# Decay masks of the state space groups fed from rows that a DMA spreads, and indexer pairs placed two units apart

## The chip, the core and the metric

The kernel runs on one core of one Trainium2 chip. A core has five engines that run their own instruction streams and meet only at semaphores: TensorE (PE in the tables; its weight loads are listed apart as PEld), VectorE (DVE), ScalarE (ACT), GpSimd (POOL) and SyncE (SP), which here only issues DMAs. The metric is the device time of one execution in microseconds (us), lower is better.

## The reference, cut to what matters

One encoder block: a feed-forward half step, a mixer, a second feed-forward half step, on 256 tokens of width 2048 in float32. The change lies in the mixer, in the state space branch and in the indexer of the attention branch:

```python
u = hn @ w_in
z, xbc, dt_raw, q, k, v, q_idx, k_idx, w_idx, gate_logits = _split_cols(u)
# state space branch: 32 heads in 8 groups of 4, state 128, head width 64
acum = jnp.cumsum(ac, axis=1)                      # ac = dt * a, one number for each token and head
seg = acum[:, :, None] - acum[:, None, :]
decay = jnp.exp(jnp.where(causal, seg, -jnp.inf))
cb = jnp.einsum('btgn,bsgn->btsg', cc, bc)
y_diag = jnp.einsum('btsg,btsgr,bsgrp->btgrp', cb, decay, xc)
# indexer: 16 heads of width 64, then the 64 best keys of each query
rel = jax.nn.relu(jnp.einsum('bthd,bsd->bths', qib, k_idx))
score = jnp.einsum('bths,bth->bts', rel, wb) * idx_scale
_, sel = lax.top_k(score, top_k)
```

The kernel does not scan over chunks of 64: for each group it builds the whole decay matrix from source token s to target token t in three blocks of 128x128 for each head (first half to first half, first half to second half, second half to second half) and multiplies once.

## The kernel before

**Weight units.** All large products stream their weights. A unit is 128 x 1024 float32 (512 KB). SP loads it into one of 4 `raw` buffers (L630) once VectorE has split the unit four earlier; ScalarE copies it to the high part `w_hi` (`cast`, L834) once TensorE has finished the unit four earlier; VectorE forms the low part `w_lo` (`sub`, L1298); TensorE then runs high*high, low*high and high*low, 12 matmuls of 512 columns for a unit with tokens on the partitions (`unit`, L2075 to L2077) or 24 of 256 columns for one with features on the partitions (`fm_unit`, L2376 to L2378). So VectorE can be at most some three units ahead of TensorE.

**The order of the side work.** Units are numbered; every engine walks the same numbers and has its side work written in at fixed ones. The mixer's input product takes 8 units for each block of 512 columns: b at 264, 274; c at 282, 290; xs at 298, 306, 314, 322; z at 330, 338, 346, 354; qi at 362, 370; k at 378; v at 386; q at 394, 402, 410, 418. Through unit 361 VectorE also adds up the modulation vectors (`ada_add`, L1318, weights loaded by L636) in about 10 of 16 units, with a `fold` at the end of each of them.

**A state space group g** starts at unit s = `ssd_start[g]` = 338, 346, 354, 362, 370, 378, 386, 394.
- TensorE at s: `ssd_products` makes the products of c and b (psum bank 4) and, with 8 small matmuls, the cumulated sums of the group's four heads (bank 5 and 6): the stationary operand is one column of `dta` broadcast over 128 columns, so that every partition gets the same row of cumulated sums. At s+5 `ssd_y` multiplies; at s+10 `turn_y` transposes, which first waits until the masks of group g+1 have left bank 4 (`seg_ready`).
- VectorE at s+2: `ssd_segments`, 12 operations of 128 columns that subtract the partition's own sum `acum` and cap at zero, from psum into `decay` (L1799), then three that take the products out of psum into `cb` (L1801 to L1803). At s+4 `ssd_mask`, at s+7 `ssd_gate`, at s+9 the norm, at s+12 `y_lo_out`.
- ScalarE at s+3: `decay_exp`, one exponential over all 1536 columns (L1160).

**The indexer** has 8 pairs of heads. Pair j: TensorE at `index_slot[j]` (4 matmuls into bank 5 and 6, after `rel_ready` j), ScalarE two units later (`index_relu`, after `score_step` 4j), VectorE three units later (`index_add`, four operations). The pairs stand at units 381 to 384 and 389 to 392; since they share banks 5 and 6 with the cumulated sums, `ssd_products` of groups 6 and 7 waits for `rel_ready` 4 and `head_ready`, and `index` for `seg_ready` 6 or 7. At 396 VectorE runs `admit`, and from 397 one of eight top-8 rounds a unit.

**Once, at unit 290**, `cumulate` makes the sums with tokens on the partitions (`acum`).

Of the kernel before, what the change touches and what calls it, by code (L numbers as in the profile page):

```python
# [113 lines left out]
def build(nc, x, c, positions, w_ada, b_ada, norm_ffn1, ffn1_w1, ffn1_w3, ffn1_w2, norm_mix, w_in,  # L114
# [94 lines left out]
    zs = place("zs", at_temp + 36 * KB, [GROUPS, HALF, T])  # L209
    yT_hi = place("yT_hi", at_temp + 20 * KB, [KT, T], F32R)  # L210
# [37 lines left out]
    gate_dram = nc.dram_tensor("gate_rows", (3, KT, P), F32).ap()  # L248
    h_dram = nc.dram_tensor("h_spill", (P, HALF, D), F32).ap()
# [80 lines left out]
    cb_ready = sem("cb_ready")  # L330
    seg_ready = sem("seg_ready")
# [60 lines left out]
    index_slot = ([start[at_block["k"]] + 3 + j for j in range(4)] + [start[at_block["v"]] + 3 + j for j in range(4)])  # L392
# [232 lines left out]
    def _(sp):  # L625
# [18 lines left out]
        for f in range(2):  # L644
# [32 lines left out]
            for n in range(MIX, M0):  # L677
                if n in FRONT_UNITS:
                    s = At(n).slot(RAW)
                    rows = slice((n - FRONT) * FRONT_KT * P, (n - FRONT + 1) * FRONT_KT * P)  # L680
                    dst = raw[:, s, 0:FRONT_KT * FRONT_COLS].rearrange("p (k n) -> p k n", k=FRONT_KT)
                    sp.wait_ge(split_ready, n + 1 - RAW)
                    sp.dma_start(dst[:, :, 0:SSD_H],
                                 w_in[0][rows, DT0:DT0 + SSD_H].rearrange("(k p) n -> p k n", p=P)).then_inc(front_in[n - FRONT], 16)
                    sp.dma_start(dst[:, :, SSD_H:],
                                 w_in[0][rows, KI0:G0].rearrange("(k p) n -> p k n", p=P)).then_inc(raw_in[s], 16)
                    continue
                load_unit(At(n), mix_source(n))
                if mixed_ada(n):
                    e, k = mixed_ada(n)  # L690
                    load_ada(At(e * KT + k), ada_source(e, k))
# [110 lines left out]
    def _(act):  # L802
# [277 lines left out]
        def xs_out(b):  # L1080
            i = WBLOCKS[b][1]
            act.wait_ge(xs_turned, i + 1)
            for half in range(HALF):
                ins = nc.scalar.activation(xs[:, 2 * i:2 * i + 2, half, :], by_group(4 + half), ACT.Copy)
            ins.then_inc(xs_ready, 1)
# [71 lines left out]

        def decay_exp(g):
            act.wait_ge(seg_ready, g + 1)
            nc.scalar.activation(decay[:], decay[:], ACT.Exp).then_inc(decay_ready, 1)  # L1160
# [49 lines left out]
        def mixer():  # L1210
            for n in range(MIX, M1):
                cast_units(n + 1)
                for b in range(NW):
# [18 lines left out]
                    if kind[b] == "k" and n == end[b] + 9:  # L1232
                        k_out()
# [6 lines left out]
                if n == FRONT_END + 11:  # L1240
                    kiT_out()
                for g in range(GROUPS):
                    s = ssd_start[g]
                    if n == s + 3:
                        decay_exp(g)
                    if n == s + 8:
                        y_square(g)
                    if n == s + 12:
                        y_hi_out(g)
# [42 lines left out]
    def _(dve):  # L1292
# [496 lines left out]
        def ssd_segments(g):  # L1789


            dve.wait_ge(cb_ready, g + 1)
# [4 lines left out]
            for j, bank, col in ((0, 5, 0), (1, 6, 2), (2, 6, 1)):  # L1797
                for k in range(4):
                    nc.vector.tensor_scalar(decay[:, j, k, :], psum[:, bank, k * P:(k + 1) * P],  # L1799
                                            acum[:, col, 4 * g + k:4 * g + k + 1], 0.0, ALU.add, ALU.min)  # L1800
# [172 lines left out]
        def mixer():  # L1973
            for n in range(MIX, M1):
# [14 lines left out]
                if n == FRONT_END + 2 * UPB + 2:  # L1989
                    cum_out()  # L1990
# [70 lines left out]
    def _(pe):  # L2061
# [339 lines left out]
        def turn_xs(b):  # L2401
            pe.wait_ge(conv_out, b + 1)
            i = WBLOCKS[b][1]
            if i:
                pe.wait_ge(xs_ready, i)
            for half in range(HALF):
                for k in range(4):
                    ins = turn(psum[:, 4 + half, k * P:(k + 1) * P], conv[:, k, half * P:(half + 1) * P])
            ins.then_inc(xs_turned, 1)

        def cumulate():

            pe.wait_ge(dta_ready, 1)
            pe.wait_ge(front_read, 1)
            for half in range(HALF):
                plain(psum[:, 4, half * SSD_H:(half + 1) * SSD_H], upper[:], dta[:, half, :])
            plain(psum[:, 4, 64:96], ones[:], dta[:, 0, :]).then_inc(cum_ready, 1)

        def ssd_products(g):
# [7 lines left out]
            if g == 6:  # L2427
                pe.wait_ge(rel_ready, 4)
            if g == 7:
                pe.wait_ge(head_ready, 1)  # L2430
            plain(psum[:, 4, 0:T], bT[:, g, 0:P], cT[:, g, :])
            plain(psum[:, 4, T:T + P], bT[:, g, P:T], cT[:, g, P:T])
            for half in range(HALF):
                for k in range(4):
                    ins = plain(psum[:, 5 + half, k * P:(k + 1) * P],
                                dta[:, half, 4 * g + k:4 * g + k + 1].broadcast_to((P, P)), upper[:])
            ins.then_inc(cb_ready, 1)
# [21 lines left out]
        def index(j):  # L2459
# [8 lines left out]
            pe.wait_ge(seg_ready, 6 if j < 4 else 7)  # L2468
# [79 lines left out]
        def mixer():  # L2548
            for n in range(MIX, M0):
                for b in range(NW):  # L2550
                    if kind[b] == "xs" and n == end[b] + 7:
                        turn_xs(b)
                    if kind[b] == "k" and n == end[b] + 7:
# [16 lines left out]
                if n == FRONT_END + 2 * UPB:  # L2570
# [107 lines left out]
```

## Time and profile before

| | |
|---|---|
| median of 3 runs | 2574.16 us (2573.16 to 2575.64) |
| the profiled execution | 2575.62 us, of which the span from first to last instruction 2573.9 us |
| PE busy | 2523.1 us, 98% |
| DVE busy | 1846.8 us, 72% |
| ACT busy | 1151.3 us, 45% |
| mean granted TensorE clock | 0.996 |

The span and what lies outside it (1.7 us) make up the profiled execution, which is 1.5 us above the median. A row's "busy" adds up the durations of instructions; those of matmuls overlap. Units 338 to 405 lie at about 1026 to 1275 us of the span.

### The profile page before, as it was taken

Reading aid. Unit: us, or ns where it says so; the run is one execution under the profiler, and the core shown is the slowest. Engines: PE = TensorE matmul, PEld = TensorE weight load, DVE = VectorE, ACT = ScalarE, POOL = GpSimd, SP = SyncE. Lnnn points to the kernel's source line nnn. Section 1 sums busy time; section 2 is a strip of 40 time slices with the busy share of each in tenths; the row PEclk is TensorE's granted clock in tenths of the full one; section 3 lists DMA queues with packets and bytes.
Section 4 is the critical chain, followed back from the end, with each engine's and each line's share of the span. In section 5 each row is a group of like instructions: output and inputs, shape, how many; then the busy total and the mean of one; then the engine's idle time right before and its main releaser. Section 6 shows DMA issues by size and latency. Waiting matters only on the chain.

```text
span 2573.9 us, 33768 instructions
## 1 busy us (share of the span) xinstructions
PE 2523.1 (98%) x12444; PEld 2127.6 (83%) x12444; DVE 1846.8 (72%) x2028; ACT 1151.3 (45%) x1365; POOL 114.2 (4%) x136
## 2 busy tenths in 40 slices
PE   7999999999998999999999999999999999999999
PEld 5878888888887999898788888887788888888887
DVE  5876678888976978967866677776779655555556
ACT  4444444344445555544455444443544444444443
POOL 4210000000002000000000000000300000000000
PEclk9999999999999999999999999999999999999999
DMA  9976679898977787654454788786499666666665
GB/s 372 384 249 194 188 264 344 293 342 293 343 238 227 246 293 262 212 164 124 143 145 138 229 277 263 256 288 231 133 314 336 192 191 189 191 190 189 192 190 173
DMA packets 279997, 610.15 MB, mean 237 GB/s; under 512 B 23426, under 2 KB 24004, under 8 KB 278980
## 3 DMA queue, kind: packets, MB, share of 16 engines
q1 hardware_dynamic: 268432, 567.22, 67.8%
q0 software_dynamic: 9744, 36.73, 3.8%
q10 hardware_dynamic: 1700, 4.58, 0.5%
q8 instruction: 77, 1.26, 0.2%
q14 instruction: 44, 0.36, 0.0%
HBM read 604.24 MB, written 4.22 MB: 236 GB/s over the span
## 4 chain that ended last, share of the span: by engine, by line
PE 90%; DVE 5%; DMA 2%; issue 1%; ACT 1%; POOL 0%; ACTq 0%; DVEq 0%; POOLq 0%
PE psum L2075 25%; PE psum L2077 25%; PE psum L2076 25%; PE psum L2376 3%; PE psum L2377 3%; PE psum L2378 3%; PE psum L2399 2%; PE psum L2063 2%; DMA raw<-in_ffn_w 1%; DVE w_lo L1298 1%; DVE ada_acc L1412 0%; DVE decay L1799 0%; ACT w_hi L834 0%; DVE score L1874 0%; DVE ada_acc L1318 0%
## 5 line engine op out<-in xcount | busy, mean ns | idle before, releaser
L1298 DVE TENSOR_TENSOR w_lo<-raw,w_hi 128x1024 fp32r<-128x1024 f32 x850 | 1034.8, 1222 | 524.3 <-ACT w_hi L834 523.3
L834 ACT ACTIVATE w_hi<-raw 128x1024 fp32r<-128x1024 f32 x850 | 897.6, 1060 | 1016.4 <-PE psum L2077 879.1
L2075 PE MATMUL psum<-w_hi,xT_hi 128*128 128x512 f32 x1984 | 785.6, 396 | 9.1 <-DVE w_lo L1298 4.0
L2077 PE MATMUL psum<-w_hi,xT_lo 128*128 128x512 f32 x1984 | 774.0, 390 | 0.0
L2076 PE MATMUL psum<-w_lo,xT_hi 128*128 128x512 f32 x1984 | 773.6, 390 | 0.0
L2075 PEld LDWEIGHTS psum<-w_hi,xT_hi 128*128 128x128 f32 x1984 | 373.4, 188 | 91.7 <-issue 15.3
L2077 PEld LDWEIGHTS psum<-w_hi,xT_lo 128*128 128x128 f32 x1984 | 373.1, 188 | 78.8
L2076 PEld LDWEIGHTS psum<-w_lo,xT_hi 128*128 128x128 f32 x1984 | 373.8, 188 | 75.8
L2075 PE MATMUL psum<-w_hi,aT_hi 128*128 128x512 f32 x704 | 274.8, 390 | 0.0
L2077 PE MATMUL psum<-w_hi,aT_lo 128*128 128x512 f32 x704 | 274.1, 389 | 0.0
L2076 PE MATMUL psum<-w_lo,aT_hi 128*128 128x512 f32 x704 | 274.0, 389 | 0.0
L1318 DVE SCALAR_TENSOR_TENSOR ada_acc<-ada_raw,cact,ada_acc 128x1024 f32<-128x1024 f32 x210 | 269.4, 1283 | 0.1
L2376 PE MATMUL psum<-xT_hi,w_hi 128*128 128x256 f32 x640 | 182.8, 286 | 6.3 <-DVE xT_lo L1457 5.7
L2377 PE MATMUL psum<-xT_lo,w_hi 128*128 128x256 f32 x640 | 181.1, 283 | 0.0
L2378 PE MATMUL psum<-xT_hi,w_lo 128*128 128x256 f32 x640 | 181.1, 283 | 0.0
L2077 PEld LDWEIGHTS psum<-w_hi,aT_lo 128*128 128x128 f32 x704 | 132.1, 188 | 27.6
L2075 PEld LDWEIGHTS psum<-w_hi,aT_hi 128*128 128x128 f32 x704 | 132.2, 188 | 27.4
L2076 PEld LDWEIGHTS psum<-w_lo,aT_hi 128*128 128x128 f32 x704 | 132.2, 188 | 27.2
L1517 DVE TENSOR_TENSOR y<-psum,y 128x1024 f32<-128x1024 f32 x93 | 113.6, 1221 | 31.5 <-PE psum L2077 31.5
L2376 PEld LDWEIGHTS psum<-xT_hi,w_hi 128*128 128x128 f32 x640 | 122.5, 191 | 7.5 <-DVE xT_lo L1457 6.5
L2377 PEld LDWEIGHTS psum<-xT_lo,w_hi 128*128 128x128 f32 x640 | 122.5, 191 | 0.0
L2378 PEld LDWEIGHTS psum<-xT_hi,w_lo 128*128 128x128 f32 x640 | 122.5, 191 | 0.0
(258 smaller groups left out, 1974.5 us busy)
## 6 DMA issues: line engine op xcount, KB each, us to landing
raw<-in_ffn_w SPq DMA_DIRECT2D x528, 512.0 KB, 4.5
ada_raw<-in_w_ada SPq DMA_DIRECT2D x224, 512.0 KB, 5.9
raw<-in_w_in SPq DMA_DIRECT2D x224, 512.0 KB, 3.9
ada_raw<-in_w_ada POOLq DMA_DIRECT2D x32, 512.0 KB, 7.5
ada_more<-in_w_ada POOLq DMA_DIRECT2D x32, 512.0 KB, 7.6
raw<-in_w_br_ssd SPq DMA_DIRECT2D x32, 512.0 KB, 5.2
raw<-in_w_br_att SPq DMA_DIRECT2D x32, 512.0 KB, 4.7
raw<-in_w_out SPq DMA_DIRECT2D x32, 512.0 KB, 5.4
```

Source lines behind the costliest of these rows:

```text
L834: nc.scalar.activation(w_hi[:, n.slot(SPLIT), 0:size], raw[:, n.slot(RAW), 0:size], ACT.Copy).then_inc(hi_ready, 1)
L1298: nc.vector.tensor_tensor(w_lo[:, n.slot(SPLIT), 0:size], raw[:, n.slot(RAW), 0:size], w_hi[:, n.slot(SPLIT), 0:size], ALU.subtract).then_ ...
L1318: nc.vector.scalar_tensor_tensor(out=acc[:], in0=src, scalar=cact[:, k:k + 1], in1=acc[:], op0=ALU.mult, op1=ALU.add).then_inc(ada_used, 1)
L1517: nc.vector.tensor_tensor(y[:, :, cols], psum[:, bank:bank + HALF, :], y[:, :, cols], ALU.add).then_inc(y_added, 1)
L2063: return nc.tensor.transpose(dst, src, ident[0:rows_, 0:rows_])
L2075: nc.tensor.matmul(o, hi[:, kt + k, toks], whi, start=a, stop=False)
L2076: nc.tensor.matmul(o, hi[:, kt + k, toks], wlo, start=False, stop=False)
L2077: ins = nc.tensor.matmul(o, lo[:, kt + k, toks], whi, start=False, stop=b)
L2376: nc.tensor.matmul(o, w_hi[:, s, cols], xT_hi[:, kt + k, :], start=a, stop=False, skip_group_check=True)
L2377: nc.tensor.matmul(o, w_hi[:, s, cols], xT_lo[:, kt + k, :], start=False, stop=False, skip_group_check=True)
L2378: ins = nc.tensor.matmul(o, w_lo[:, s, cols], xT_hi[:, kt + k, :], start=False, stop=b, skip_group_check=True)
L2399: return nc.tensor.matmul(o, a, b, start=first, stop=last)
```

## The change

The cumulated sums are made once, as 32 rows (one for each head) of 256 tokens: `cumulate` has two more products of `dta` (stationary) and `upper`, ScalarE copies them out (`cum_copy`, unit 292) and stores them to DRAM with a DMA of its own. For each group SP loads the group's four rows, 4 KB, into all 128 partitions (`cum_spread`, two buffers, 512 KB for each load), placed ahead of the load of unit s-2. The 8 matmuls for each group go. The first-to-second-half block, whose differences are never positive, goes to ScalarE as four exponentials with `acum` as the bias (`decay_off`); VectorE keeps 8 of its 12 operations, now from SBUF, and waits for TensorE's products only after them. The remaining exponential covers 1024 columns. The indexer pairs move to units 379, 381, ..., 393; the waits between them and the groups go, since banks 5 and 6 have no other user now, and the turn of k moves from unit 393 to 396.

```diff
-    index_slot = ([start[at_block["k"]] + 3 + j for j in range(4)] + [start[at_block["v"]] + 3 + j for j in range(4)])
+    index_slot = [start[at_block["k"]] + 1 + 2 * j for j in range(8)]
+    CUM_AT = FRONT_END + 2 * UPB
...
             for n in range(MIX, M0):
+                for g in range(GROUPS):
+                    if n == ssd_start[g] - 2:
+                        if g == 0:
+                            sp.wait_ge(cum_stored, 16)
+                        if g >= 2:
+                            sp.wait_ge(off_ready, g - 1)
+                            sp.wait_ge(seg_ready, g - 1)
+                        sp.dma_start(cum_spread[:, g % 2], cum_dram[4 * g:4 * g + 4, :].rearrange("(o r) n -> o r n", o=1)
+                                     .broadcast_to((P, 4, T))).then_inc(cum_in[g % 2], 16)
...
+        def cum_copy():
+
+            act.wait_ge(cum_ready, 1)
+            nc.scalar.activation(cum_rows[0:SSD_H, :], psum[0:SSD_H, 5, 0:T], ACT.Copy).then_inc(cum_copied, 1)
+            act.wait_ge(cum_copied, 1)
+            act.dma_start(cum_dram, cum_rows[0:SSD_H, :]).then_inc(cum_stored, 16)
+
+        def decay_off(g):
+
+            act.wait_ge(cum_in[g % 2], 16 * (g // 2 + 1))
+            act.wait_ge(acum_ready, 1)
+            if g:
+                act.wait_ge(y_raw, g)
+                act.wait_ge(masked_ready, g)
+            for k in range(4):
+                ins = nc.scalar.activation(decay[:, 1, k, :], cum_spread[:, g % 2, k, P:T], ACT.Exp,
+                                           bias=acum[:, 2, 4 * g + k:4 * g + k + 1])
+            ins.then_inc(off_ready, 1)
+
         def decay_exp(g):
+            decay_off(g)
             act.wait_ge(seg_ready, g + 1)
-            nc.scalar.activation(decay[:], decay[:], ACT.Exp).then_inc(decay_ready, 1)
+            nc.scalar.activation(decay[:, 0:3:2], decay[:, 0:3:2], ACT.Exp).then_inc(decay_ready, 1)
...
-            dve.wait_ge(cb_ready, g + 1)
+            dve.wait_ge(cum_in[g % 2], 16 * (g // 2 + 1))
             dve.wait_ge(acum_ready, 1)
             if g:
                 dve.wait_ge(y_raw, g)
                 dve.wait_ge(masked_ready, g)
-            for j, bank, col in ((0, 5, 0), (1, 6, 2), (2, 6, 1)):
+            for half in range(HALF):
                 for k in range(4):
-                    nc.vector.tensor_scalar(decay[:, j, k, :], psum[:, bank, k * P:(k + 1) * P],
-                                            acum[:, col, 4 * g + k:4 * g + k + 1], 0.0, ALU.add, ALU.min)
+                    nc.vector.tensor_scalar(decay[:, 2 * half, k, :], cum_spread[:, g % 2, k, half * P:(half + 1) * P],
+                                            acum[:, half, 4 * g + k:4 * g + k + 1], 0.0, ALU.add, ALU.min)
+            dve.wait_ge(cb_ready, g + 1)
...
             pe.wait_ge(dta_ready, 1)
+            pe.wait_ge(kiT_ready, 1)
             pe.wait_ge(front_read, 1)
             for half in range(HALF):
                 plain(psum[:, 4, half * SSD_H:(half + 1) * SSD_H], upper[:], dta[:, half, :])
+            for half in range(HALF):
+                plain(psum[0:SSD_H, 5, half * P:(half + 1) * P], dta[:, half, :], upper[:])
...
-            if g == 6:
-                pe.wait_ge(rel_ready, 4)
-            if g == 7:
-                pe.wait_ge(head_ready, 1)
             plain(psum[:, 4, 0:T], bT[:, g, 0:P], cT[:, g, :])
-            plain(psum[:, 4, T:T + P], bT[:, g, P:T], cT[:, g, P:T])
-            for half in range(HALF):
-                for k in range(4):
-                    ins = plain(psum[:, 5 + half, k * P:(k + 1) * P],
-                                dta[:, half, 4 * g + k:4 * g + k + 1].broadcast_to((P, P)), upper[:])
-            ins.then_inc(cb_ready, 1)
+            plain(psum[:, 4, T:T + P], bT[:, g, P:T], cT[:, g, P:T]).then_inc(cb_ready, 1)
...
-            pe.wait_ge(seg_ready, 6 if j < 4 else 7)
...
-                    if kind[b] == "k" and n == end[b] + 7:
+                    if kind[b] == "k" and n == end[b] + 10:
                         turn_k(b)
```

TensorE's queue around units 389 to 394 before (`kiT,qiT` is a pair of the indexer, `ident,qn` the turn of k, `cT,bT` the products of group 7, `upper,dta` its cumulated sums; between the marks stand the unit's own matmuls):

```order
L2399 MATMUL psum<-xdt,decay 128x64 x12
L2399 MATMUL psum<-kiT,qiT 128x256 x4
L2075 MATMUL psum<-w_hi,xT_hi 128x512
...
L2063 MATMUL psum<-ident,qn 128x128 x8
L2075 MATMUL psum<-w_hi,xT_hi 128x512
...
L2399 MATMUL psum<-cT,bT 128x256
L2399 MATMUL psum<-cT,bT 128x128
L2399 MATMUL psum<-upper,dta 128x128 x8
L2075 MATMUL psum<-w_hi,xT_hi 128x512
```

The same place in the changed kernel:

```order
L2440 MATMUL psum<-xdt,decay 128x64 x12
L2440 MATMUL psum<-kiT,qiT 128x256 x4
L2116 MATMUL psum<-w_hi,xT_hi 128x512
...
L2440 MATMUL psum<-cT,bT 128x256
L2440 MATMUL psum<-cT,bT 128x128
L2116 MATMUL psum<-w_hi,xT_hi 128x512
...
L2104 MATMUL psum<-ident,qn 128x128 x8
L2104 MATMUL psum<-ident,yg_137 128x128 x4
```

The eight `upper,dta` are gone, and the turn of k stands behind the products of group 7 now.

VectorE's queue before, from unit 394 to the start of 397 (`score` is the indexer's sum, `cb` and `decay` belong to group 7, `banned` and `dist` to `admit`):

```order
L1874 SCALAR_TENSOR_TENSOR score<-rel,wi,score 128x256 x4
L1298 TENSOR_TENSOR w_lo<-raw,w_hi 128x1024
L1838 TENSOR_SCALAR yg_135<-yg,y_rstd 128x256 x2
L1874 SCALAR_TENSOR_TENSOR score<-rel,wi,score 128x256 x4
L1298 TENSOR_TENSOR w_lo<-raw,w_hi 128x1024
L1799 TENSOR_SCALAR decay<-psum,acum 128x128 x12
L1801 TENSOR_TENSOR cb<-psum,upper 128x128
L1802 COPY cb<-psum 128x128
L1803 TENSOR_TENSOR cb<-psum,upper 128x128
L1893 TENSOR_SCALAR banned<-key_chunk,query_chunk 128x256 x2
```

And in the changed kernel:

```order
L1915 SCALAR_TENSOR_TENSOR score<-rel,wi,score 128x256 x4
L1338 TENSOR_TENSOR w_lo<-raw,w_hi 128x1024
L1879 TENSOR_SCALAR yg_137<-yg,y_rstd 128x256 x2
L1338 TENSOR_TENSOR w_lo<-raw,w_hi 128x1024
L1839 TENSOR_SCALAR decay<-cum_spread,acum 128x128 x8
L1842 TENSOR_TENSOR cb<-psum,upper 128x128
L1843 COPY cb<-psum 128x128
L1844 TENSOR_TENSOR cb<-psum,upper 128x128
L1915 SCALAR_TENSOR_TENSOR score<-rel,wi,score 128x256 x4
L1934 TENSOR_SCALAR banned<-key_chunk,query_chunk 128x256 x2
```

The last pair's sum now stands behind the masks of group 7, right ahead of `admit`, and four of the twelve mask operations are gone.

SP's queue at the first of the eight new loads:

```order
L638 DMA raw<-in_w_in 128x2x512
L693 DMA cum_spread<-cum_rows 128x1024
L638 DMA raw<-in_w_in 128x2x512
L644 DMA ada_raw<-in_w_ada 128x1024
L638 DMA raw<-in_w_in 128x2x512
```

The new load stands between two weight loads of the same queue.

## Rows read from the trace of the kernel before

**Rows 1.** The page: busy time (share) and instructions; the chain by engine.
```profile
PE 2523.1 (98%) x12444; PEld 2127.6 (83%) x12444; DVE 1846.8 (72%) x2028; ACT 1151.3 (45%) x1365; POOL 114.2 (4%) x136
...
PE 90%; DVE 5%; DMA 2%; issue 1%; ACT 1%; POOL 0%; ACTq 0%; DVEq 0%; POOLq 0%
```

**Rows 2.** Windows: us, then PE, PEld, DVE, ACT, POOL busy (count), clock, DMA share, GB/s.
```profile
860.00:1000.00 140.00, 140.00 (x1171) 140.00 (x1170) 120.95 (x173) 74.63 (x96) 0.00 (x0) 1.00 0.79 265
...
1020.00:1060.00 40.00, 40.00 (x212) 34.31 (x211) 34.54 (x59) 21.02 (x27) 1.78 (x2) 1.00 0.81 276
...
1026.10:1300.00 273.90, 268.34 (x1571) 231.62 (x1570) 217.44 (x407) 132.30 (x184) 16.21 (x22) 1.00 0.54 164
...
1053.46:1081.00 27.54, 27.54 (x147) 23.53 (x146) 23.91 (x39) 14.96 (x20) 1.76 (x2) 1.00 0.72 233
```

**Rows 3.** Timeline around group 0: start, us, engine, line, names [idle before, releaser].
```profile
1026.10 0.85 PEld L2399 LDWEIGHTS psum<-cT,bT 128*128 128x128 f32 x4
...
1026.87 1.87 PEld L2399 LDWEIGHTS psum<-upper,dta 128*128 128x128 f32 x16
...
1028.66 0.19 PEld L2075 LDWEIGHTS psum<-w_hi,xT_hi 128*128 128x128 f32 x1
...
1028.97 3.19 DVE L1799 TENSOR_SCALAR decay<-psum,acum 128x128 f32<-128x128 f32 x12 [1.88 <-PE psum L2399]
...
1032.79 1.49 ACT L1160 ACTIVATE decay<-decay 128x1536 f32<-128x1536 f32 x1 [2.93 <-DVE cb L1803]
```

**Rows 4.** TensorE's timeline, units 355 to 404: the waits that another engine ended.
```profile
1089.39 0.30 PE L2063 MATMUL psum<-ident,yg 128*128 128x128 f32 x1 [0.54 <-DVE cb L1803]
...
1192.33 0.49 PE L2399 MATMUL psum<-kiT,qiT 64*128 64x256 f32 x2 [0.26 <-ACT rel L1155]
...
1207.67 0.30 PE L2063 MATMUL psum<-ident,yg 128*128 128x128 f32 x1 [0.61 <-DVE cb L1803]
...
1227.80 0.49 PE L2399 MATMUL psum<-kiT,qiT 64*128 64x256 f32 x2 [2.10 <-ACT rel L1155]
...
1232.86 0.30 PE L2063 MATMUL psum<-ident,qn 128*128 128x128 f32 x1 [0.94 <-ACT rel L1155]
...
1263.53 0.39 PE L2076 MATMUL psum<-w_lo,xT_hi 128*128 128x512 f32 x1
1263.75 0.39 PE L2077 MATMUL psum<-w_hi,xT_lo 128*128 128x512 f32 x1
1264.87 0.47 PE L2075 MATMUL psum<-w_hi,xT_hi 128*128 128x512 f32 x1 [0.73 <-DVE w_lo L1298]
...
1274.16 0.50 PE L2075 MATMUL psum<-w_hi,xT_hi 128*128 128x512 f32 x1 [0.39 <-DVE w_lo L1298]
```

**Rows 5.** VectorE's timeline at units 395 and 396; last row: two scalings in SBUF.
```profile
1235.36 1.67 DVE L1874 SCALAR_TENSOR_TENSOR score<-rel,wi,score 128x256 f32<-128x256 f32 x4
...
1239.16 3.20 DVE L1799 TENSOR_SCALAR decay<-psum,acum 128x128 f32<-128x128 f32 x12 [0.99 <-PE psum L2399]
...
1077.95 0.60 DVE L1838 TENSOR_SCALAR yg<-yg,y_rstd 128x256 f32<-128x256 f32 x2
```

**Rows 6.** DMA issues, KB, us to landing; last row: all DMAs of gate_rows.
```profile
raw<-in_w_in SPq DMA_DIRECT2D x64, 512.0 KB, 3.7
ada_raw<-in_w_ada SPq DMA_DIRECT2D x10, 512.0 KB, 6.0
...
DMA to landing us min/median/max: 3.3/6.3/8.3
```

**Rows 7.** Groups by form: xcount, busy us, mean ns, idle before.
```profile
L1165 ACT ACTIVATE yg<-yg 128x256 f32<-128x256 f32 x14 | 5.7, 412 | 15.4 <-DVE yg L1833 15.4
...
L834 ACT ACTIVATE w_hi<-raw 128x1024 fp32r<-128x1024 f32 x65 | 68.4, 1057 | 36.0 <-PE psum L2077 21.4 <-PE psum L2378 14.4
```

**Rows 8.** Windows behind the mixer, at the half-clock stretch.
```profile
1790.00:1795.00 5.00, 2.60 (x10) 2.11 (x11) 1.94 (x6) 2.17 (x4) 0.61 (x1) 0.50 0.40 118
1795.00:1800.00 5.00, 5.00 (x13) 3.85 (x13) 0.74 (x1) 0.00 (x0) 0.28 (x1) 0.50 0.95 397
```

More of the change, by code:

```diff
@@ L209, in build @@
     zs = place("zs", at_temp + 36 * KB, [GROUPS, HALF, T])
+    cum_rows = place("cum_rows", at_temp + 22 * KB, [T])
+    cum_spread = place("cum_spread", at_temp + 76 * KB, [2, 4, T])
     yT_hi = place("yT_hi", at_temp + 20 * KB, [KT, T], F32R)
@@ L248, in build @@
     gate_dram = nc.dram_tensor("gate_rows", (3, KT, P), F32).ap()
+    cum_dram = nc.dram_tensor("cum_rows", (SSD_H, T), F32).ap()
     h_dram = nc.dram_tensor("h_spill", (P, HALF, D), F32).ap()
@@ L330, in build @@
     cb_ready = sem("cb_ready")
+    cum_copied = sem("cum_copied")
+    cum_stored = sem("cum_stored")
+    cum_in = [sem("cum_in0"), sem("cum_in1")]
+    off_ready = sem("off_ready")
     seg_ready = sem("seg_ready")
@@ L1082, in xs_out @@
             act.wait_ge(xs_turned, i + 1)
+            act.wait_ge(cum_stored, 16)
             for half in range(HALF):
@@ L1231, in mixer @@
                             head_squares(1 + WBLOCKS[b][1], b)
-                    if kind[b] == "k" and n == end[b] + 9:
+                    if kind[b] == "k" and n == end[b] + 12:
                         k_out()
@@ L1241, in mixer @@
                     kiT_out()
+                if n == CUM_AT + 2:
+                    cum_copy()
                 for g in range(GROUPS):
@@ L1988, in mixer @@
                     dt_rest(n - FRONT_END - 7)
-                if n == FRONT_END + 2 * UPB + 2:
+                if n == CUM_AT + 2:
                     cum_out()
@@ L2403, in turn_xs @@
             i = WBLOCKS[b][1]
-            if i:
-                pe.wait_ge(xs_ready, i)
+            pe.wait_ge(xs_ready, i) if i else pe.wait_ge(cum_copied, 1)
             for half in range(HALF):
@@ L2569, in mixer @@
                     ins.then_inc(ki_turned, 1)
-                if n == FRONT_END + 2 * UPB:
+                if n == CUM_AT:
                     cumulate()
```

## The prediction

> **What bounds the kernel now.** I read the page first: TensorE is busy for 98% of the span and carries 90% of the chain that ended last [rows 1]. Then the windows over the changed stretch, units 338 to 405: of 273.9 us TensorE is busy for 268.3, VectorE for 217.4, ScalarE for 132.3, at full granted clock [rows 2]. Then TensorE's timeline, for what it waits for there: seven waits, 5.57 us in all [rows 4]. Three end with ScalarE's `rel` (0.26, 2.10, 0.94), the chain of an indexer pair in which TensorE, ScalarE and VectorE take turns at one unit's distance; two with VectorE's `cb` (0.54, 0.61), where `turn_y` waits for the masks of the next group; two with `w_lo` (0.73, 0.39), where VectorE is truly the bound, in the top-8 rounds. So in this stretch a matmul removed is time removed, as long as VectorE keeps up, and five of the seven waits belong to chains that the change touches.
>
> A rule speaks against reading it so. The Trainium skill, Perfetto Trace Analysis, section Identifying the Most-Contended Engine, says that matmul busy time is a poor measure of headroom and that LDWEIGHTS busy should be used; that is 231.6 of 273.9 us here, so by it TensorE would have 42 us free and a removal might bring nothing. It is rival D below; the trace doesn't side with it, since the waits add up to 5.57 us only.
>
> **The change part by part.**
>
> *The eight small matmuls of each group go.* Around group 0 their weight loads begin at 1026.87 and the next unit's first one at 1028.66 [rows 3]: 1.79 us for 8 matmuls (16 records, two for each). Nothing lies over them: TensorE goes straight on. 8 groups x 1.79 = **14.3 us off the path**.
>
> By the Trainium skill, TensorE: Matmul & The Clock Gate, section Back-to-back issue gap, matmuls of 128 columns follow each other at about 81 ns; 8 x 16 of them would be an estimated 10.4 us. The trace's own distance, 112 ns, is what I use.
>
> *Added on TensorE:* two more products in `cumulate`, 128 columns each, four records at the same 0.112 us: 0.45 us, taken as **0.5 us added**. Its new wait for `kiT_ready` names a step that ScalarE does five units earlier: nothing.
>
> *The waits in which TensorE stood for the pairs and masks* [rows 4]. The three with `rel`: a unit is 12 matmuls, 0.22 us apart (starts 1263.53 and 1263.75), so 2.7 us. A pair now has two units (5.5 us) until the next instead of one, and what must fit between is one ScalarE relu of 1024 columns (as a cast of as many, 1.06 us [rows 7]), the four sums of 1.67 us [rows 5], and the unit's own cast and split, 1.06 and 1.2. That is 5.0 in a row: too long for 2.7, short enough for 5.5. The turn of k, which waits for the last pair, moves back three units. The two with `cb`: VectorE's mask work for a group was 3.19 us after a wait for TensorE's products (1.88 us at group 0, 0.99 at group 7) [rows 3, 5]. Now it need not wait and does 8 of 12 operations. So I let all five go: 4.45 us, and with each the refill of the pipeline. That shows at the wait of 0.73 us: starts 1263.75 and 1264.87 are 1.12 apart where 1263.53 and 1263.75 are 0.22 apart, so the stop costs 0.9, 0.17 more than the wait. 5 x 0.16 = 0.8. Together **5.25 us**; the bounds are 0 (other turns come last, rival B) and 5.25.
>
> *VectorE's share, at the two waits with `w_lo`.* An operation from psum costs 3.19 / 12 = 0.27 us. From SBUF the trace has the same operation with twice the columns at 0.60 for two, 0.30 each [rows 5]. So one of 128 columns costs at most 0.27 and at least half of it, 0.13; I take 0.2, nearer the wider SBUF row less its columns. 8 x 0.2 = 1.6 against 3.2: 1.6 us less a group (bounds 1.1 and 2.1). In the stretch to 1264 VectorE gains the 0.99 wait and 1.6, but the last pair's sum (1.67) now stands inside it, behind the masks of group 7, while TensorE arrives 1.79 earlier. Counted from the same split that is 0.9 gained against 1.79 needed: the wait would grow by 0.9. But that split began at 1236.95 only because the pair's sum at 1235.36 had just ended [rows 5]; with the sum moved, it can begin up to 1.6 us sooner. Net 0.7 better. The two waits with refill are 1.44 us; I take half, **0.7 us**, with 0 and 1.44 as bounds, and down to -1 if the split does not come sooner.
>
> *ScalarE.* The one exponential of 1490 ns becomes four of 128 columns and one of 1024. 256 columns take 412 ns and 1024 take 1057 [rows 7], so 128 take about 0.3: 1.2 + 1.06, 0.8 us more a group. The four lie in the 2.93 us in which ScalarE waited for the masks [rows 3]; behind them stand the casts of the next units, which get 0.4 us earlier. Cost nothing; without that cover 0.8 x 8 on an engine that is half idle. Once, at unit 292, `cum_copy` and its DMA issue, 0.4 us by the row of 256 columns [rows 7] and an issue that has no row, say up to 1 us: ScalarE is busy for 75 of 140 us there and TensorE for all of it [rows 2]. Nothing.
>
> *SP and the DMAs.* Eight more loads of 512 KB, 4.2 MB. Same size: 3.7 us to landing for weights, 6.0 for the modulation's, and 8.3 for the slowest of the gate rows, the only transfers here that spread small DRAM rows over the partitions [rows 6]. The new load stands behind the load of unit s-3, which waits for the split of s-7, and it is read at s+2: nine units, 24 us. SP's own new waits name masks two groups old; the weight loads queued behind them are not held. The DMA engines are busy for 0.81 of the time in the fullest window [rows 2]; a load for every 8 units adds under 0.1. Nothing; what it costs if the spread is slow is rival E.
>
> *Sum:* 14.3 - 0.5 + 5.25 + 0.7 = 19.75 us. From the profiled execution, 2573.9 span + 1.7 around it = 2575.6, that gives 2555.9; the shown median is 1.5 lower, so **2554.4 us**.
>
> **The rivals.**
>
> A, the forecast, 2554.4; own range 2552.5 to 2557. Chance 0.62.
>
> B, the matmuls' time comes but the waits don't: VectorE is the next engine. For it: in the window of groups 1 and 2 it is busy for 23.9 of 27.5 us [rows 2], and TensorE's share shrinks to 25.7; against it: its own shrinks to some 22.3. Without the 5.95 us of waits: 2574.2 - 13.8 = 2560.4, up to 2562. Chance 0.18.
>
> C, the clock behind the mixer. From 1790 to 1800 the granted clock is 0.50, the lower of its two levels (1.2 GHz); TensorE is idle for 2.4 of the first 5 us and works for 7.6 of the 10 [rows 8], so the stretch costs 3.8 us. Shifted by 20 us it may fall elsewhere or not at all: 2550.6, or 2558.2 if it gets longer. Chance 0.12.
>
> D, the change takes work from an engine that has room: 2574. For it only PEld's 85%, against it the sum of waits. Chance 0.04.
>
> E, slower: all partitions read the same 4 KB. Unit n's weights are asked for when n-4 is split, at best three units (8.2 us) ahead, and take 3.7, so 4.5 us are spare. If a spread holds the queue for x us, TensorE stops for x - 4.5 each time. Gain and loss balance at x = 4.5 + 19.75 / 8 = 7.0; at 8.3, the slowest of rows 6, it is 8 x 3.8 = 30 us: 2585. Against it: that row holds twice the bytes in 512 B pieces. Chance 0.04.
>
> **How the numbers follow.** The likeliest case gives 2554.4. The range reaches over C's gain and B's loss: 2550.5 to 2562.5, which leaves out D, E and the ends of A to C, under 2 in 10. About 0.2% (5 us) is what a measurement of this kernel can tell from no change; A, B and C all lie beyond it: faster 0.92, same 0.04 (D), slower 0.04 (E).
>
> **What would show it.** In the profile after, TensorE's timeline should have the next unit's first weight load some 0.7 us behind the start of each group's products, not 2.5; no wait for `rel`, and none for `cb`; VectorE's masks in 1.6 us or so with no wait for TensorE ahead; the spread loads landing within 8 us and no cast that waits for a weight DMA in this stretch. A wait for `w_lo` longer than 1 us between 1230 and 1270 would speak for B, a half-clock stretch of another length behind the mixer for C, casts released by a weight DMA at the groups for E. The forecast is wrong if VectorE's operations from SBUF cost as much as from psum and the stops in the top-8 rounds grow.

## The result, and the profile after

The changed kernel takes **2555.15 us** (median of 4 runs, 2553.68 to 2555.81); the kernel before, run beside it, 2573.93 (4 runs, 2573.16 to 2575.64). The ratio is 0.9925 (95% interval 0.9913 to 0.9937): faster by 0.75%, 18.8 us. The forecast was 2554.4.

The page of the changed kernel, busy time and chain by engine, against [rows 1]:

```profile
PE 2507.5 (98%) x12320; PEld 2113.5 (83%) x12320; DVE 1834.7 (72%) x1996; ACT 1158.0 (45%) x1398; POOL 114.0 (4%) x136
...
PE 91%; DVE 5%; DMA 2%; issue 1%; ACT 1%; POOL 0%; ACTq 0%; DVEq 0%; POOLq 0%
```

TensorE and VectorE have less to do (15.6 and 12.1 us), ScalarE more (6.7), and TensorE still carries the chain.

**Where the time went.** The records of single products mark points of the two traces. Products of `c` and `b` and logits (`kT,qT`), before: name, count, ns, first and last start.

```profile
L2399 PE MATMUL psum<-kT,qT x64: 377/379/382, 1289.0 to 1404.4; 128*128 128x256 f32 x64
...
L2399 PE MATMUL psum<-cT,bT x32: 271/326/381, 1026.3 to 1237.1; 128*128 128x256 f32 x16, 128*128 128x128 f32 x16
```

The same in the changed kernel, with the products of `cumulate`:

```profile
L2440 PE MATMUL psum<-kT,qT x64: 377/379/382, 1268.7 to 1384.1; 128*128 128x256 f32 x64
...
L2440 PE MATMUL psum<-cT,bT x32: 271/326/381, 1025.8 to 1218.9; 128*128 128x256 f32 x16, 128*128 128x128 f32 x16
...
L2440 PE MATMUL psum<-upper,dta x4: 272/273/297, 884.5 to 884.8; 128*32 128x128 f32 x4
```

From the products of group 0 to the first logits, which I call **the stretch** below, it is 1289.0 - 1026.3 = 262.7 us before and 1268.7 - 1025.8 = 242.9 after: 19.8 us. The forecast has one term ahead of the stretch, the added products in `cumulate` at unit 290. To take it in, count from the first turned block of activations (`ident,act_tok`, at 190.1 us before and 188.9 after), which lies ahead of all that was changed: to the first logits it is 1098.9 us before and 1079.8 after, **19.1 us** for the whole change, against 19.75 in the forecast. (The two profiled executions, 2575.62 and 2555.07, lie 20.55 apart, of which 1.2 us arose ahead of 190 us, where the two kernels do the same; the medians lie 18.8 apart. The last section says where totals move while these distances don't.)

Windows of the changed kernel, as in [rows 2] and [rows 8]: us, PE, PEld, DVE, ACT, POOL busy (count), clock, DMA share, GB/s.

```profile
1020.00:1060.00 40.00, 40.00 (x198) 33.72 (x197) 35.18 (x56) 26.08 (x38) 1.77 (x2) 1.00 0.89 310
1026.10:1281.00 254.90, 253.82 (x1447) 218.19 (x1446) 205.41 (x375) 139.89 (x219) 15.98 (x22) 1.00 0.59 190
...
1770.00:1775.00 5.00, 2.72 (x13) 2.01 (x14) 2.51 (x4) 2.17 (x4) 0.61 (x1) 0.58 0.64 204
1775.00:1780.00 5.00, 5.00 (x18) 4.00 (x17) 0.00 (x0) 1.06 (x1) 0.56 (x1) 0.74 0.85 345
```

In these windows over the groups and the indexer TensorE is idle for 1.1 us, where it was for 5.6. The fullest window's DMA share rose from 0.81 to 0.89. The stretch at the lower clock behind the mixer is still there, but the second window is already back at 0.74 where it was 0.50: it lasts 6.8 us instead of 10.2.

Timeline around group 0 of the changed kernel, against [rows 3]:

```profile
1025.61 0.84 PEld L2440 LDWEIGHTS psum<-cT,bT 128*128 128x128 f32 x4
1025.83 0.81 PE L2440 MATMUL psum<-cT,bT 128*128 128x256 f32 x4
1026.37 0.19 PEld L2116 LDWEIGHTS psum<-w_hi,xT_hi 128*128 128x128 f32 x1
...
1026.50 1.65 DVE L1839 TENSOR_SCALAR decay<-cum_spread,acum 128x128 f32<-128x128 f32 x8
...
1029.37 1.28 ACT L1191 ACTIVATE decay<-cum_spread,acum 128x128 f32<-128x128 f32 x4
1030.56 1.05 ACT L1198 ACTIVATE decay<-decay 128x1024 f32<-128x1024 f32 x1
```

The next unit's first weight load stands 0.76 us behind the products' first one, where it stood 2.56 behind (1026.10 and 1028.66 in [rows 3]): 1.80 less. VectorE's masks take 1.65 us instead of 3.19 and have no wait ahead of them; ScalarE's four exponentials take 1.28 and the wide one 1.05, instead of 1.49 in one.

All of TensorE's waits for other engines in the stretch, against the seven of [rows 4]; each line ends with total us, times, longest.

```profile
PE psum L2104 <- DVE cb L1844: 0.8, 1, 0.8
PE psum L2116 <- DVE w_lo L1338: 0.3, 1, 0.3
```

**The sum closes.** The eight groups' matmuls are worth 14.3 us (8 x 1.79). The waits, each with the 0.16 of refill that the prediction takes from the wait of 0.73, were 5.57 + 7 x 0.16 = 6.7 before and are 0.81 + 0.27 + 2 x 0.16 = 1.4 after, so 5.3. Together that is 19.6 of the 19.8.

**The one wait that stayed** is the turn of group 1's `y` at unit 356, and it grew from 0.54 to 0.81. VectorE's timeline there, changed kernel; the last row is TensorE's:

```profile
1075.28 1.23 DVE L1338 TENSOR_TENSOR w_lo<-raw,w_hi 128x1024 fp32r<-128x1024 f32 x1 [0.96 <-ACT w_hi L851]
1076.42 1.28 DVE L1358 SCALAR_TENSOR_TENSOR ada_acc<-ada_raw,cact,ada_acc 128x1024 f32<-128x1024 f32 x1
1077.73 0.45 DVE L1376 STREAM_TRANSPOSE fold_tmp<-ada_acc 128x256 f32<-128x256 f32 x1
...
1081.36 1.65 DVE L1839 TENSOR_SCALAR decay<-cum_spread,acum 128x128 f32<-128x128 f32 x8
...
1083.32 0.28 DVE L1844 TENSOR_TENSOR cb<-psum,upper 128x128 f32<-128x128 f32 x1
...
1083.74 0.63 PE L2104 MATMUL psum<-ident,yg 128*128 128x128 f32 x4 [0.81 <-DVE cb L1844]
```

And the same place before:

```profile
1085.13 0.42 DVE L1339 TENSOR_REDUCE fold_s<-fold_tmp 128x8 f32<-128x256 f32 x1
1085.46 3.18 DVE L1799 TENSOR_SCALAR decay<-psum,acum 128x128 f32<-128x128 f32 x12
...
1088.96 0.28 DVE L1803 TENSOR_TENSOR cb<-psum,upper 128x128 f32<-128x128 f32 x1
```

Here the masks never waited for TensorE's sums: in both kernels they stand right behind the `fold`, 3.6 us of small operations. So from this group VectorE gets only 3.18 - 1.65 = 1.53 us, while TensorE gets 1.79. The difference, 0.26, is what the wait grew by (0.27).

### The profile page after: what moved, and what is told of

It is laid out like the page before. It is cut to its first block, busy times and chain, and to the rows that moved or that the text cites. A ratio compares the mean times of both kernels' runs of the same rounds, so it can differ in the third digit from the quotient of the medians.

```text
span 2553.3 us, 33548 instructions
## 1 busy us (share of the span) xinstructions
PE 2507.5 (98%) x12320; PEld 2113.5 (83%) x12320; DVE 1834.7 (72%) x1996; ACT 1158.0 (45%) x1398; POOL 114.0 (4%) x136
## 4 chain that ended last, share of the span: by engine, by line
PE 91%; DVE 5%; DMA 2%; issue 1%; ACT 1%; POOL 0%; ACTq 0%; DVEq 0%; POOLq 0%
PE psum L2116 26%; PE psum L2117 26%; PE psum L2118 26%; PE psum L2417 3%; PE psum L2419 3%; PE psum L2418 3%; PE psum L2440 2%; PE psum L2104 2%; DVE w_lo L1338 1%; DVE ada_acc L1452 0%; DMA raw<-in_ffn_w 0%; DMA gate_ffn<-gate_rows 0%; DMA badas<-in_b_ada 0%; DVE ada_acc L1358 0%; PE psum L2197 0%
```

## The experiments

"Ratio" is against the kernel before on the same chip, with its 95% interval; "again" runs repeat a kernel. The stretch is given for each, since it repeats closely: 262.7 and 263.0 before, 242.9 and 243.0 for the changed kernel, where totals of one kernel in one series lie up to 7.7 us apart (e5).

### e1: the changed kernel with the pairs where they were

```diff
-    index_slot = [start[at_block["k"]] + 1 + 2 * j for j in range(8)]
+    index_slot = ([start[at_block["k"]] + 3 + j for j in range(4)] + [start[at_block["v"]] + 3 + j for j in range(4)])
```

The waits between pairs and groups stay away, and the turn of k stays at unit 396.

> The changed kernel with the indexer pairs back at units 381 to 384 and 389 to 392, without the waits between pairs and groups. Theory (the distance of two units is what removed the waits for rel): the waits of TensorE for rel come back, 0.26 + 2.10 and the one at the turn of k gone since that stays three units later; about 2.5 us slower than the changed kernel, near 2557.7. Rival (the shared psum banks and their waits made the chain long, the distance does nothing): no wait for rel, within 0.5 us of the changed kernel, near 2555.

Measured: 2560.26 us (2559.68 to 2560.61), ratio 0.9945 (0.9928 to 0.9961); stretch 247.5, **4.6 longer** than the changed kernel's. The direction was as expected, the size nearly double. TensorE's waits in the stretch, e1:

```profile
PE psum L2440 <- ACT rel L1173: 1.9, 2, 1.7
PE psum L2104 <- DVE cb L1844: 1.7, 2, 0.9
PE psum L2116 <- DVE w_lo L1338: 0.2, 1, 0.2
```

The `rel` waits are back though the shared banks and their waits are not, so the rival falls. Back is also a second `cb` wait, which I had put down to the masks alone. The two long ones in TensorE's timeline of e1:

```profile
1195.33 0.63 PE L2104 MATMUL psum<-ident,yg 128*128 128x128 f32 x4 [0.88 <-DVE cb L1844]
...
1215.05 1.14 PE L2440 MATMUL psum<-kiT,qiT 64*128 64x256 f32 x8 [1.67 <-ACT rel L1173]
```

It was 0.61 before and is 0.88 here: again 0.27 more, the same 1.79 against 1.53. On VectorE the sum of a pair (1.67 us) stands close ahead of those masks, in the kernel before and in e1, with only a split and a reduction between them; in the changed kernel it stands behind them, and the wait is gone. VectorE's masks there in the kernel before, with no wait ahead of them, then the changed kernel's with the pair's sum behind:

```profile
1199.90 1.67 DVE L1874 SCALAR_TENSOR_TENSOR score<-rel,wi,score 128x256 f32<-128x256 f32 x4
...
1203.75 3.18 DVE L1799 TENSOR_SCALAR decay<-psum,acum 128x128 f32<-128x128 f32 x12
```

```profile
1190.07 1.65 DVE L1839 TENSOR_SCALAR decay<-cum_spread,acum 128x128 f32<-128x128 f32 x8
...
1192.23 1.66 DVE L1915 SCALAR_TENSOR_TENSOR score<-rel,wi,score 128x256 f32<-128x256 f32 x4
```

### e8: e1 once more

> The kernel with the pairs back at one unit's distance, profiled once more. In the first profile the granted clock fell to 0.50 for 3.4 us at 1217 us, 2 us after TensorE had waited 1.67 us for rel, and that cost 1.4 us on top of the waits. Theory (the wait brings the fall about): it falls there again. Rival (chance): it does not, and the stretch is 246.1 us instead of 247.5.

Measured: 2561.58 us (one run); stretch 247.5 again. The clock did not fall there, so the wait alone does not bring the fall about; but the stretch isn't the 246.1 expected without it either. Its waits in the stretch:

```profile
PE psum L2440 <- ACT rel L1173: 1.9, 2, 1.7
PE psum L2104 <- DVE cb L1844: 1.7, 2, 0.9
PE psum L2116 <- DVE w_lo L1338: 1.5, 2, 1.1
```

The waits for `w_lo` are 1.5 us against 0.2 in e1, and yet the stretch is equal. In e1 the granted clock fell 1.4 us behind the end of the wait of 1.67 and was low for 3.4 us, from 1216.5 to 1219.9. A window over most of it in e1, then one around the same wait (1.65) in e8:

```profile
1217.00:1220.40 3.40, 3.40 (x11) 2.64 (x10) 1.78 (x5) 1.53 (x3) 1.06 (x2) 0.58 0.54 151
```

```profile
1215.00:1225.00 10.00, 8.35 (x42) 6.46 (x41) 5.68 (x12) 6.86 (x14) 1.25 (x2) 1.00 0.22 63
```

At the half clock e1's matmuls are 0.43 us apart instead of 0.22. Up to this wait e8's records run 2.06 us behind e1's, at the products of group 7 (1223.27 and 1223.74) only 0.47, and at the logits 2.0 again. So what TensorE lost by the fall, 1.6 us, it got back in the top-8 rounds, where it waits less for VectorE: the fall cost nothing, and VectorE sets the end of this part. In e8, where no fall blurs it, the waits with refill sum to 5.12 + 6 x 0.16 = 6.1, against 1.4: 4.7, the 4.6 measured. It splits into 2.2 for `rel` (1.9 and two refills), 1.0 for the second `cb`, and the rest for `w_lo`.

### e2: the small matmuls back, for four groups

Groups 0 to 3 run their eight matmuls again, into banks that nobody reads.

```diff
-            plain(psum[:, 4, T:T + P], bT[:, g, P:T], cT[:, g, P:T]).then_inc(cb_ready, 1)
+            ins = plain(psum[:, 4, T:T + P], bT[:, g, P:T], cT[:, g, P:T])
+            if g < 4:
+                for half in range(HALF):
+                    for k in range(4):
+                        ins = plain(psum[:, 5 + half, k * P:(k + 1) * P],
+                                    dta[:, half, 4 * g + k:4 * g + k + 1].broadcast_to((P, P)), upper[:])
+            ins.then_inc(cb_ready, 1)
```

> The changed kernel with the 8 small matmuls put back for groups 0 to 3 alone, into psum banks that nobody reads, so only their time on TensorE is added. Theory (TensorE is the bound there, each group's matmuls cost their 1.79 us in full): 4 x 1.79 = 7.2 us slower than the changed kernel, near 2562.3, less 0.5 to 1 where the wait at the turn of group 1 absorbs it. Rival (TensorE has room, as its weight load share of 83% would have it): under 2 us slower.

Measured: 2561.09 us (2558.95 to 2565.42), ratio 0.9946 (0.9929 to 0.9963); stretch 249.2, 6.3 longer. The records of e2 (64 in the groups, 4 in `cumulate`):

```profile
L2440 PE MATMUL psum<-upper,dta x68: 272/275/297, 887.5 to 1113.1; 128*128 128x128 f32 x64, 128*32 128x128 f32 x4
```

4 x 1.79 = 7.2 us of matmuls cost 6.3, and the `cb` wait at unit 356 (0.81 + 0.16) is gone: TensorE is late enough not to meet it. The only wait left in the stretch of e2:

```profile
PE psum L2116 <- DVE w_lo L1338: 0.3, 1, 0.3
```

So 7.2 - 1.0 = 6.2 were to be expected. Work on TensorE is time here, one for one; rival D falls.

### e3: the middle block back on VectorE

```diff
-            for half in range(HALF):
+            for j, half, col in ((0, 0, 0), (1, 1, 2), (2, 1, 1)):
...
-            nc.scalar.activation(decay[:, 0:3:2], decay[:, 0:3:2], ACT.Exp).then_inc(decay_ready, 1)
+            nc.scalar.activation(decay[:], decay[:], ACT.Exp).then_inc(decay_ready, 1)
```

(the masks' sources change with it, and the four biased exponentials and SP's wait for them go).

> The changed kernel with the middle block of the masks back on VectorE, 12 operations from SBUF, and one exponential of 1536 columns on ScalarE. Theory (VectorE has room but in two places): 4 x 0.2 = 0.8 us more on VectorE a group; the wait of TensorE for the masks at unit 356 grows by up to 0.8 and the one in the top-8 rounds by up to 0.8, so 0.8 to 1.6 us slower, near 2556.4. Rival (VectorE is the next bound everywhere): 8 x 0.8 = 6.4 us slower, 2561.5. Rival (ScalarE's four exponentials hold its casts up): as fast or faster than the changed kernel.

Measured: 2555.26 us (2552.88 to 2557.58), ratio 0.9929 (0.9913 to 0.9946); stretch 244.5, 1.6 longer. The total can't tell it from the changed kernel, the stretch can. Waits of e3:

```profile
PE psum L2098 <- DVE cb L1838: 1.6, 1, 1.6
PE psum L2110 <- DVE w_lo L1332: 0.8, 2, 0.5
```

The masks take 2.44 us for twelve, 0.8 more than eight, and the `cb` wait grows by just that, 0.81 to 1.60; the waits for `w_lo` grow from 0.3 to 0.8. Giving the block to ScalarE is worth 1.6 us, at these two places only; at the other groups no wait came up, so VectorE has slack there.

### e4: two spreads instead of eight

Only groups 0 and 1 have their sums loaded; the others form their masks with the sums of group 0 or 1, so those masks are not their own.

```diff
-                for g in range(GROUPS):
+                for g in range(2):
...
-            act.wait_ge(cum_in[g % 2], 16 * (g // 2 + 1))
+            act.wait_ge(cum_in[g % 2], 16)
...
-            dve.wait_ge(cum_in[g % 2], 16 * (g // 2 + 1))
+            dve.wait_ge(cum_in[g % 2], 16)
```

> The changed kernel with the spread loads of groups 0 and 1 only; the other groups read these again, so their masks are not those of their own heads. Theory (the loads are hidden): within 0.5 us of the changed kernel, near 2555. Rival (they delay weight loads): each of the 6 removed loads gives back time, over 1 us together.

Measured: 2554.34 us (2553.98 to 2554.67), ratio 0.9922 (0.9906 to 0.9939); stretch 242.9, exactly the changed kernel's. Six loads of 512 KB less bring nothing: they are hidden.

### e5: the spreads late

```diff
-                    if n == ssd_start[g] - 2:
+                    if n == ssd_start[g] + 5:
```

> The changed kernel with each spread load placed ahead of the weight load of unit s+5 instead of s-2, seven units later. It is then issued when the unit s has been split and is read two splits later. Theory (slack of nine units before, a landing of 4.6 to 8.5 us): now VectorE waits for it at the masks, 1 to 4 us a group, and its lead of up to three units over TensorE takes most of it: 0 to 8 us slower than the changed kernel, by the stretch's own time. If it is within 0.5 us even so, the lead alone would carry a spread that is late by seven units, and the rival by which slow spreads make the change a loss has no ground. If it is over 15 us slower, that rival was nearer than the prediction held.

Measured: 2556.91 us (2553.95 to 2561.62), ratio 0.9929 (0.9913 to 0.9946); stretch 243.4, 0.5 longer. VectorE's timeline, e5, groups 0 and 1:

```profile
1036.45 1.66 DVE L1839 TENSOR_SCALAR decay<-cum_spread,acum 128x128 f32<-128x128 f32 x8 [4.35 <-DMA cum_spread<-cum_rows]
...
1060.66 1.66 DVE L1839 TENSOR_SCALAR decay<-cum_spread,acum 128x128 f32<-128x128 f32 x8 [1.83 <-DMA cum_spread<-cum_rows]
```

Now VectorE does stand for the load, 6.2 us in all, at the first two groups only; for the other six it has no such wait. TensorE loses 0.5, all of it around these two groups, 0.1 of it at the `cb` wait at unit 356 (0.93 instead of 0.81). That VectorE's lead over TensorE takes the rest is how I read it. So the placement could slip by seven units at hardly any cost.

### e6 and e7: can the waits that are left be taken away?

e6 turns `y` one unit later, so that `cb` is surely done; e7 also starts `admit` and the top-8 rounds two units later, behind the last pair.

```diff
-                if n == s + 10:
+                if n == s + 11:
...
-                    if n == s + 12:
+                    if n == s + 13:
```

```diff
-                if n == s + 2:
+                if n == s + 4:
...
-                if s + 3 <= n < s + 3 + TOPK // 8:
+                if s + 5 <= n < s + 5 + TOPK // 8:
```

(the first is e6, the second what e7 adds, with `top_out` two units later too; the first stands for TensorE's turn, its second line for both halves of the output).

> The changed kernel with the turn of each group's output at unit s+11 instead of s+10 and what follows it (high and low part) at s+13 instead of s+12. Theory (the one wait for the masks that stayed, 0.81 us at unit 356, is VectorE late behind its fold, and a unit more is enough): no wait for cb, the stretch from the first group's products to the first logits 0.9 to 1.0 us shorter, 242.0 instead of 242.9 us. Rival (ScalarE, which waits for the turn a unit later, delays its casts): new waits for w_lo, the stretch not shorter.

e6: 2556.09 us (2554.56 to 2557.40), ratio 0.9932 (0.9915 to 0.9948); stretch 241.8, 1.1 shorter: the 0.81 and its refill, and 0.1 at the wait for `w_lo`. The only wait left in the stretch of e6:

```profile
PE psum L2116 <- DVE w_lo L1338: 0.2, 1, 0.2
```

> As the kernel with the later turn, and with admit at unit 398 instead of 396 and the top-8 rounds at 399 to 406 instead of 397 to 404. Theory (the wait for w_lo at the end of the rounds, 0.27 us and its refill, is VectorE's backlog): it goes too, stretch 241.5 us, total 1.4 us under the changed kernel, 2553.8. Rival (the backlog only moves to the turn of q and the first logits): stretch as with the later turn alone or longer.

e7: 2553.23 us (2552.68 to 2553.93), ratio 0.9919 (0.9903 to 0.9936); stretch 241.2, and TensorE waits for no engine in it.

### e9, e10, e11: the changed kernel, e7 and the kernel before, again on one chip

> The changed kernel once more, on the same chip as the next, for a direct comparison. Theory (the stretch from the first group's products to the first logits tells a kernel's share, the rest of the span varies with the stretches of half clock): stretch 242.9 us again within 0.1, total within 2 us of 2555.2. Rival (the stretch itself varies by a microsecond or more): another length.

> The kernel with the later turn and the later rounds, beside the changed kernel. Theory: stretch 241.2 us, 1.7 us under the changed kernel, and the total as much; with 5 rounds that is at the edge of what can be told. Rival (the first difference of 1.9 us was half clock luck): totals the same though the stretch is shorter.

> The kernel before, profiled once more. Theory: the stretch takes 262.7 us again within 0.3, so that the 19.8 us between the two profiles are the change's and what lies ahead of the stretch (0.5 us earlier) is chance. Rival: the waits for rel or the half clock vary, stretch 1 us or more off.

e9: 2554.23 us (2552.33 to 2557.47, 5 runs), ratio 0.9925 (0.9911 to 0.9938), stretch 243.0. e10: 2553.10 (2552.09 to 2554.75, 5 runs), ratio 0.9922 (0.9908 to 0.9935), stretch 241.1. e11: 2574.98 (one run), stretch 263.0. The stretches repeat to 0.3 us, and e7's is 1.7 to 1.9 shorter than the changed kernel's in both pairs. In the totals it is 1.1 us faster in this pair, inside the spread of both: the stretch shows e7's gain, the totals don't.

e11 had its own fall of the clock, right behind a wait of 2.08 us that is 2.10 in the first trace of before and brought none there:

```profile
1227.95 1.13 PE L2399 MATMUL psum<-kiT,qiT 64*128 64x256 f32 x8 [2.08 <-ACT rel L1155]
```

A window over most of it in e11, and the turn of k behind it:

```profile
1229.60:1233.00 3.40, 3.40 (x11) 2.68 (x10) 2.08 (x5) 1.25 (x4) 1.25 (x2) 0.59 0.52 140
```

```profile
1233.43 1.03 PE L2063 MATMUL psum<-ident,qn 128*128 128x128 f32 x8
```

The wait of 0.94 us for `rel` that stood ahead of this turn in the first trace is gone here: the fall took its place, and from the pair to the turn it is 5.48 us instead of 5.06, 0.4 longer.

## Why the prediction held, step by step

- **What bounds the kernel: right.** e2 shows it: 7.2 us of matmuls put back cost 6.3, and the missing part is a wait that they covered. The rule on LDWEIGHTS busy (the Trainium skill, Perfetto Trace Analysis, Identifying the Most-Contended Engine) would have seen 42 us of room here; this measurement decides against it as a measure of slack in this stretch.
- **14.3 us for the matmuls: right.** After group 0's products the next unit's follow 1.80 us sooner. e2 prices 64 of these records at 6.3 + 1.0 = 7.3 us, 114 ns each; with the 81 ns of the Trainium skill (TensorE: Matmul & The Clock Gate, Back-to-back issue gap) it would be an estimated 5.2.
- **0.5 added in `cumulate`: a little small.** From there to group 0 the changed kernel's lead shrinks from 1.2 to 0.5 us, and all of this 0.7 lies in `cumulate` itself: from its first product to the next unit's matmul it is 0.59 us before (885.17 to 885.76) and 1.26 after (884.01 to 885.27). The four new records take 0.55 to the next one, 0.14 each instead of the 0.11 taken from the groups' records, and the four ahead of them 0.46 instead of 0.36.
- **"So I let all five go": four went.** The `rel` waits did, by the pairs' spacing, as reckoned. Of the two `cb` waits one stayed. The step that failed is "Now it need not wait and does 8 of 12 operations": at unit 356, and in [rows 4] the wait of 0.61 too, VectorE had not been waiting for TensorE's sums. There the masks gain 1.53 us against TensorE's 1.79, so by itself the change makes both waits longer, and the second went for another reason, the pair's sum moved from ahead of it. Instead of 1.5 gained with refill, 0.5 came: 0.77 gone, 0.27 grown.
- **0.7 for the two `w_lo` waits: too careful.** 1.44 became 0.43, a gain of 1.0. The masks' step from SBUF is 0.2 as taken (eight in 1.65). What the pairs' move does here was reckoned the right way round but only as a net of 0.7: e8, with the pairs where they were, has 1.8 us of these waits with refill and the changed kernel 0.4, so the move is worth 1.4 and the rest of the change costs 0.4.
- **The total: partly luck.** The error at the `cb` waits is -1.0 and the one at `w_lo` +0.3. For the stretch, without the term of `cumulate`, the forecast was 20.25; less 0.7 that is 19.6, and 19.8 were measured; with `cumulate`, 19.75 against 19.1. That the median lies only 0.8 us from the forecast says little, since totals of one kernel move by more.
- **ScalarE at no cost: right.** 6.7 us more on the page, 0.8 a group as worked out, and TensorE has no wait for ScalarE in the stretch. A block of 128 columns takes 394 ns; the Trainium skill (ScalarE: Activation LUTs, What ACT_TABLE_LOAD costs) has 280 + 0.833 x 128 = 387 for an operation with such a bias, and the trace agrees.
- **The spreads at no cost: right**, by e4 (six fewer, same stretch) and e5 (seven units later, 0.5 us). They land like other loads of their size, so rival E had no ground. Rows of the changed kernel: the issues, and their landing in us:

```profile
L693 SPq DMA_DIRECT2D cum_spread<-cum_rows x8: 358/412/1453, 999.5 to 1184.6; - x8
...
DMA to landing us min/median/max: 4.6/5.8/8.5
```

- Three of its signs did not hold: "none for `cb`"; "landing within 8 us", where the slowest took 8.5; and "no cast that waits for a weight DMA". Three casts of the stretch wait, 5.2 us together, all at 1248 us or later, some 60 us behind the last spread, and TensorE waits for none of them, as the list of waits shows. The last was no sign to begin with: the kernel before has four such waits there, 7.2 us.
- **Rival B** would have been 2560.4. That is nearly what e1 gives (2560.26) without the pairs' move: the spacing of the pairs, one line of the change, decides between it and the forecast. **Rival C** came in part: the half-clock stretch behind the mixer is 6.8 us long instead of 10.2. No effect of the change is shown by it: the kernel before has 10.2 in its first trace and 6.8 in e11.

## What to carry to other kernels

Taking work off the bounding engine makes it arrive earlier at every engine that it meets; compare, at each meeting, what both sides save (here 1.79 against 1.53 us), before you write a wait off. When two edits come together, ask of each wait which of the two removes it: moving the pairs was worth a quarter of this gain (4.6 of 19.8 us, e1). And read a change of under 1% from the distance between two fixed points of the trace, which repeated to 0.3 us here where whole runs of one kernel lay up to 7.7 apart.

## What the runs showed of the hardware

- **The clock's falls come and go in the same kernel.** Outside the stretch each trace has other ones, near the start and behind the mixer, stretches of 3.4 to 10.2 us (one at 809 us in the changed kernel's first trace and e8, none there in e9). Behind the same wait of TensorE, 1.67 and 1.65 us, the clock fell in e1 and held in e8; behind 2.08 and 2.10 in the kernel before likewise.
- **Totals move near the start.** In the eleven traces of the changed kernel and its variants the first `ident,act_tok` starts at 186.9 to 194.5 us, 7.6 apart, though all do the same up to there; from it to group 0's products it is 836.9 or 837.0 us in every one (836.2 and 836.3 in the two of the kernel before). Behind the first logits the span left is 1282.8 to 1286.2 us. In the first 200 us the time at the lower clock adds up to 3.4 us in e4, whose block starts at 186.9, and to 13.6 in e2, where it starts at 191.9; that fits, but e5 (10.4 us, 194.5) shows that the clock is not all of it, and the rest stays open.
- **A fall can be free.** e1 and e8 have the same stretch, 247.5, with and without it, since VectorE was the later of the two at its end. In the kernel before (263.0 with, 262.7 without) the fall took the place of most of a wait for `rel`. The falls near 809 us cost nothing either: the traces with one there (e8) and without (e9) have the same 836.9 us, and the ones with it wait 4.3 instead of 5.7 us for `xT_lo`.
- **A small source spread over all partitions is no slow transfer.** 4 KB of DRAM read by 128 partitions lands in 4.6 to 8.5 us, median 5.8, beside medians of 3.6 (weights) and 5.6 (modulation) for plain loads of 512 KB in the same stretch.
